# Two output projections by seven quarter products instead of eight, and the last grid sums spread by PE

## The reference, cut to what matters

```python
# first block
mix = concatenate([na_out, ml_out], -1)        # 2048 x 1024: grid attention | mLSTM, 512 columns each
h   = x + gate * (mix @ w_out)                 # w_out 1024 x 1024
x1  = rmsnorm(h, final_norm_w)
# second block
hn  = rms_norm(x1, norm_w_2)                   # feeds the second block's projections
...
mixed = concatenate([y_f, y_a], -1) @ w_out_2  # y_f = fourier part * silu, y_a = dilated attention part
out = x1 + mixed
```

## Time and profile before

| | us |
|---|---|
| median of three runs | 3999.92 |
| profiled execution | 3991.84 |
| its span | 3990.0 |
| PE busy | 3648.1 (91%) |
| ACT, DVE, POOL busy | 1190.5, 921.9, 287.9 |
| first output projection, first matmul to last transpose | 1670.2 to 1926.9 |
| second output projection, first matmul to last | 3763.0 to 3985.2 |

### The profile page before, as it was taken

The page is one execution under the profiler, slowest core; times in us unless marked ns, Lnnn a source line. Parts: engine busy times, 40 slices in busy tenths (PEclk is TensorE's granted clock), DMA queues, the critical chain, the costliest instruction groups (busy, mean ns, idle before and its releaser), DMA issues. The chain is left out here.

```text
span 3990.0 us, 43121 instructions
## 1 busy us (share of the span) xinstructions
PE 3648.1 (91%) x17008; PEld 1955.1 (49%) x17008; DVE 921.9 (23%) x2342; ACT 1190.5 (30%) x2510; POOL 287.9 (7%) x232
## 2 busy tenths in 40 slices
PE   6398888989799999899899999999999999799899
PEld 3147483848354554444354445545454544344444
DVE  2323233232221321322122112222122212111110
ACT  3213131312231331322233445345444544211000
POOL 0101001010200000011000030003000200110000
PEclk9699898989899999999999999999999999899999
DMA  6110010000301101222140475334435604522221
GB/s 221 22 32 22 23 27 23 27 23 21 84 17 35 30 17 19 86 92 82 49 17 11 17 56 17 6 17 61 16 7 24 49 16 12 57 87 83 85 74 63
DMA packets 296935, 172.39 MB, mean 43 GB/s; under 512 B 162793, under 2 KB 263544, under 8 KB 293626
## 3 DMA queue, kind: packets, MB, share of 16 engines
q1 hardware_dynamic: 290470, 159.17, 26.2%
q10 hardware_dynamic: 6272, 10.49, 0.7%
HBM read 147.92 MB, written 21.71 MB: 43 GB/s over the span
## 5 line engine op out<-in xcount | busy, mean ns | idle before, releaser
L1702 PE MATMUL d<-hT,w 128*128 128x512 f32 x2560 | 1121.9, 594 | 8.3 <-POOL qk_w L1692 8.3
L1702 PEld LDWEIGHTS d<-hT,w 128*128 128x128 f32 x2560 | 485.1, 190 | 612.3 <-issue 602.1
L957 PE MATMUL n<-hT,wo 128*128 128x512 f32 x1024 | 454.2, 602 | 22.4 <-issue 12.0
L563 PE MATMUL m<-hT,w 128*128 128x512 f32 x768 | 341.2, 608 | 35.2 <-PEq L473 18.8
L957 PEld LDWEIGHTS n<-hT,wo 128*128 128x128 f32 x1024 | 194.8, 193 | 261.4 <-issue 249.3
L563 PEld LDWEIGHTS m<-hT,w 128*128 128x128 f32 x768 | 149.5, 195 | 224.9 <-issue 224.9
L2108 PE MATMUL f<-hT,w 128*128 128x512 f32 x512 | 222.9, 596 | 22.5 <-PEq L76 18.6
L568 PEld LDWEIGHTS m<-w,hT 128*128 128x128 f32 x2048 | 229.3, 192 | 1.9 <-issue 1.9
L568 PE MATMUL m<-w,hT 128*128 128x128 f32 x2048 | 229.3, 275 | 0.0
L1905 DVE CUSTOM_DVE_ANT_0 sneg<-d,bias 128x192 f32<-128x192 f32 (+1 forms) x384 | 109.5, 323 | 351.0 <-PE d L1736 341.3
L1865 ACT ACTIVATE sq<-d 128x512 f32<-128x512 f32 x96 | 57.2, 596 | 413.2 <-PE d L1702 413.2
(11 more groups left out here) (265 smaller groups left out, 3663.2 us busy)
## 6 DMA issues: line engine op xcount, KB each, us to landing
w<-in_w_in SPq DMA_DIRECT2D x68, 512.0 KB, 3.9
trig<-in_trig SPq DMA_DIRECT2D x16, 1024.0 KB, 5.0
ada<-in_w_ada SPq DMA_DIRECT2D x6, 2048.0 KB, 18.6
xg<-in_x ACTq DMA_DIRECT2D x4, 2048.0 KB, 24.3
rb<-r_rows SPq DMA_DIRECT2D x16, 512.0 KB, 5.5
wo<-in_w_in SPq DMA_DIRECT2D x16, 512.0 KB, 3.9
mix_ml<-in_x SPq DMA_DIRECT2D x16, 512.0 KB, 4.6
x<-mix_ml SPq DMA_DIRECT2D x16, 512.0 KB, 3.0
```

The lines of the kernel that those rows point to most:

```text
L563: last = nc.tensor.matmul(bank[n % 2][:], w[:, s % O_, k], hT[:, k, (n % 4) * TB:(n % 4 + 1) * TB], start=(k == 0), stop=(k == KC - 1))
L957: last = nc.tensor.matmul(bank[b][:], w[:, s, k], hT[:, k, tb * TB:(tb + 1) * TB], start=(k == 0), stop=(k == KC - 1))
L1702: last = nc.tensor.matmul(bank[tb][:], w[:, s, k], hT[:, k, tb * TB:(tb + 1) * TB], start=(k == 0), stop=(k == KC - 1))
```

## The change

Both projections go over pairs of tiles. A pair is A = (A11 A12; A21 A22) with the rows of tile 2j above and of tile 2j+1 below, the mLSTM (or dilated) columns left and the grid (or Fourier) columns right; B is the weight matrix in quarters of 512x512. The seven products, each four matmuls of 128x128 by 128x512, are

```diff
 class GridTail:
+    def widen(self, nc, pool):
+        pool.wait_ge(self.inv_out, 1)
+        wide = self.vT.rearrange("p (u q) -> p u q", q=h2)
+        nc.gpsimd.tensor_tensor(wide, self.fold[:, :].unsqueeze(1).broadcast_to([P, NU, h2]), self.inv[:, :].unsqueeze(2).broadcast_to([P, NU, h2]), ALU.mult).then_inc(self.inv_wide, 1)
+    def scale_last(self, nc, dve, mix, bank):
+        for c in range(NA_CG):
+            dve.wait_ge(self.inverse, c + 1)
+            nc.vector.tensor_tensor(dst, dst, src, ALU.mult).then_inc(self.scaled, 1)
+        for cols in (slice(0, TB), slice(TB, T)):
+            nc.vector.tensor_tensor(mix[:, g, cols], self.o[:, cols], mix[:, g, cols], ALU.mult).then_inc(self.mixed, 1)
 def grid_attention
+                        sp.dma_start(late.fold[:], t["fold"]).then_inc(consts, 16)
+                        sp.dma_start(late.ones[:], t["grid_ones"]).then_inc(consts, 16)
-                store_inverse(PAIRS - 1)
-                pool.wait_ge(consts, 16 * 7)        # the same on PE and ACT
+                pool.wait_ge(consts, 16 * 9)
+                pool.wait_ge(v_turned, 8 * PAIRS)
+                late.widen(nc, pool)
+                        elif g == PAIRS - 1:        # DVE, ahead of the last two write_out
+                            dve.wait_ge(exped, NU * PAIRS)
+                            nc.vector.reciprocal(late.inv[:], total[:]).then_inc(late.inv_out, 1)
 def project_first: SP
-                late.load_inverse(sp, t, PAIRS - 1)
+                sp.dma_start(gate_b[:], t["gate_row"][0, :].partition_broadcast(P)).then_inc(gate_in, 16)
                 (then tiles 0 to 3 of mix_rows and of x, norm_w_2, ident, and final_norm_w once mix_na is whole)
                 for b in range(NT):
                     sp.wait_ge(normed, b + 1)
                     (store b)
+                    if b + NS < NT:
+                        fetch(b + NS)
+                        sp.wait_ge(stored[b % NS], 16 * (b // NS + 1))
+                        sp.wait_ge(scaled, b + 1)
+                        load(b + NS)
 project_first: POOL
-                    nc.gpsimd.tensor_tensor(y[:, b % 2], y[:, b % 2], x[:, b % 2], ALU.add).then_inc(added, 1)
+                pool.wait_ge(gate_in, 16)
+                for k in CHUNKS:
+                    nc.gpsimd.tensor_tensor(w[:, k], w[:, k], gate_b[:], ALU.mult).then_inc(gated, 1)
+                (T3, T2, T4: three tensor_tensor of 128 x 2048)
+                sum_tiles(1)                        # four tensor_tensor of 128 x 512
+                for j in range(1, NJ):
+                    if j + 1 < NJ:
+                        sum_tiles(j + 1)
+                    join(j)                         # three tensor_tensor of 128 x 512
 project_first: PE
+                for c in range(NA_CG):
+                    nc.tensor.matmul(bank[4 + c][:], lhs, late.spread_rows(c), start=True, stop=True).then_inc(late.inverse, 1)
+                for m, k in enumerate(CHUNKS):      # tiles 0 and 1, plain
+                    pe.wait_ge(gated, m + 1)
+                    ...
+                for j in range(1, NJ):
+                    product(j, 1)                   # j == 1 also waits for ys >= 4
+                    turn(2 * j - 2)
+                    product(j, 2)
+                    product(j, 3)
+                    turn(2 * j - 1)
+                    (product(j, 4) to product(j, 7))
+                turn(NT - 2)
+                turn(NT - 1)
 project_first: DVE
+                (x added to the banks of tiles 0 and 1, four times 128 x 512)
+                dve.wait_ge(made, 1)
+                nc.vector.tensor_tensor(B12, B12, B11, ALU.subtract).then_inc(t1_out, 1)
+                norm(0); norm_again(0); norm(1); put(0); norm_again(1)
+                for j in range(1, NJ):
+                    (c11 first, c11, c12 first, c22 first) put(2 * j - 1) (u2, c12) norm(2 * j)
+                    (u3) norm_again(2 * j) (c21) norm(2 * j + 1) put(2 * j) norm_again(2 * j + 1)
 fourier: POOL
+                pool.wait_ge(proj, 8 * PAIRS)
+                tail.make(nc, pool, late)           # waits for wo_in 0 to 7, then T3, T2, T1, T4: 128 x 2048 each
 project_second
+        AHEAD = 3
+        ORDER = [(j, 1) for j in range(AHEAD)]
+        for j in range(NJ):
+            ORDER += [(j, i) for i in range(2, 8)] + ([(j + AHEAD, 1)] if j + AHEAD < NJ else [])
+                tail.collect(nc, act, bank, PAIRS - 1)   # ACT: the Fourier copies of the last pair
+                tail.join(nc, dve, bank, PAIRS - 1)      # DVE: its join, then
+                tail.mix_blocks(nc, dve, mix_f)          # the gate in four pieces of 512
```

More of the change, by code:

```diff
@@ L1230, in project_first, with bank_of, tile_done @@
         out = sem("a_out")
-        stored = [sem("a_stored0"), sem("a_stored1")]
+        stored = [sem(f"a_stored{i}") for i in range(NS)]
+        B11, B12 = w[:, ML:KC, 0:TB], w[:, ML:KC, TB:D]
+        B21, B22 = w[:, 0:ML, 0:TB], w[:, 0:ML, TB:D]
+        T3, T2, T4 = (mixed_w[:, i] for i in range(3))
+        NJ = NT // 2
+        CHUNKS = [0, 1, 2, 4, 5, 6, 7, 3]
+        USED = {1: 1, 2: 2, 3: 4, 4: 5, 5: 6, 6: 7}
+        def bank_of(j, i):
+            return (7 * (j - 1) + i + 3) % 6
+        def tile_done(eng, b):
+            if b < 2:
+                eng.wait_ge(ys, 2 * b + 2)
+            elif b % 2 == 0:
+                eng.wait_ge(held, 7 * (b // 2 - 1) + 6)
+            else:
+                eng.wait_ge(whole, b // 2)
+                eng.wait_ge(joined, 3 * (b // 2))
         with nc.Block() as block:
@@ new lines, in product @@
+                def product(j, i):
+                    a, c = 2 * j, 2 * j + 1
+                    cols = lambda b: [mix_na[:, k, b * P:(b + 1) * P] for k in range(ML)]
+                    ml = lambda b: [stage[:, b % NS, k] for k in range(ML)]
+                    s = lambda m: [sums[:, j % 2, m, k] for k in range(ML)]
+                    done = 4 * (j - 1)
+                    if i == 1:
+                        lhs, rhs = ml(a), B11
+                        pe.wait_ge(fetched[a % NS], 16 * (a // NS + 1))
+                        if j == 1:
+                            pe.wait_ge(late.scaled, PAIRS + 3)
+                            pe.wait_ge(ys, 4)
+                    elif i == 2:
+                        lhs, rhs = cols(a), B21
+                    elif i == 3:
+                        lhs, rhs = s(0), B12
+                        pe.wait_ge(shared_sums, done + 1)
+                        if j == 1:
+                            pe.wait_ge(t1_out, 1)
+                    elif i == 4:
+                        lhs, rhs = s(1), T2
+                        pe.wait_ge(shared_sums, done + 2)
+                        if j == 1:
+                            pe.wait_ge(made, 3)
+                    elif i == 5:
+                        lhs, rhs = s(2), B22
+                        pe.wait_ge(shared_sums, done + 4)
+                    elif i == 6:
+                        lhs, rhs = ml(c), T3
+                    else:
+                        lhs, rhs = cols(c), T4
+                    was = 7 * (j - 1) + i - 7
+                    if was >= 0:
+                        jj, ii = was // 7 + 1, was % 7 + 1
+                        if ii == 7:
+                            pe.wait_ge(whole, jj)
+                        else:
+                            pe.wait_ge(held, 7 * (jj - 1) + USED[ii])
+                    for k in range(ML):
+                        last = nc.tensor.matmul(bank[bank_of(j, i)][:], lhs[k], rhs[:, k], start=(k == 0), stop=(k == ML - 1))
+                    last.then_inc(prod, 1)
@@ L1361, in _ @@
                     nc.vector.reciprocal(st[:, b, 5:6], st[:, b, 4:5]).then_inc(recip, 1)
-                    if b > 0:
-                        put(b - 1)
+                nc.vector.memset(epst[:], EPS).then_inc(once, 1)
+                late.scale_last(nc, dve, mix_na, bank)
+                for b in range(2):
+                    dve.wait_ge(x_in[b], 16)
+                    for n in range(2):
+                        cols = slice(n * TB, (n + 1) * TB)
+                        dve.wait_ge(plain, 2 * b + n + 1)
+                        nc.vector.tensor_tensor(y[:, b, cols], bank[2 * b + n][:], y[:, b, cols], ALU.add).then_inc(ys, 1)
@@ L1393, in _ @@
                 for b in range(NT):
-                    sp.wait_ge(added, 2 * b + 2)
-                    sp.dma_start(y_dst[b], y[:, b % NX]).then_inc(stored[b % NX], 16)
+                    if b % 2 == 0:
+                        sp.wait_ge(held, 7 * (b // 2) + 5)
+                    else:
+                        sp.wait_ge(held, 7 * (b // 2) + 7)
+                        sp.wait_ge(joined, 3 * (b // 2) + 3)
+                    sp.dma_start(y_dst[b], y[b % NX]).then_inc(stored[b % NX], 16)
@@ new lines, in _ @@
+                pe.wait_ge(late.mixed, NTB * PAIRS)
+                for j, i in ORDER:
+                    if (j, i) == (0, 2):
+                        pe.wait_ge(tail.made, 4)
```

(12 more changed lines are left out.)

514 lines of the change are left out of this document (367 added, 147 removed).

## The result

The changed kernel ran in 3929.72 us (median of four runs, 3927.89 to 3934.69), against 3998.49 for the kernel before on the same chip: ratio 0.983, 95% interval 0.9813 to 0.9847, 68.8 us faster. The prediction was 3941, with 3931 to 3954 as its range: the direction and the mechanism of both projections held, the size was too small by 11 us, and the median lies 1.3 us outside the range. The profiled execution took 3927.89 us, span 3926.1.

The account below looks back on a forecast made before the run. PE's own rate was taken to bound both projections. Savings of 30.9 us in the first part and 28.1 in the second, 59 together, took the median from 3999.92 to 3941 us, range 3931 to 3954.

Parts of the forecast that it names:

- Passes: Both projections: 456 and 448 passes for 512 each, at 0.4292 us a pass, saving 24.0 and 27.5 us.
- Steady state: Inside both projections nothing else becomes late for PE; all added waits were costed at nothing.
- rival C: Projections: semaphore waits at each product halve the granted clock; 40% of passes so slowed give median 4096 us; chance 3%.
- rival D: Projections: handing back banks makes PE wait as long as the saved product, gain 8 us, median 3992; chance 1%.
- Grid attention's end and the start: From grid attention's end into the first projection: POOL's chain sets the start, `turn(0)` comes 1.9 us sooner.
- The term for the two more constants: Grid attention's begin: two more DMAs ahead of the complete constants start PE 0.95 us later.
- Rival A: First projection's start: no long DVE/POOL lock, `turn(0)` 5 us sooner, clock holds; gain 65 us, median 3935; chance 13%.
- Second projection's start: End of the Fourier stage: POOL's four weight sums end the block, and PE begins 0.9 us sooner.
- rival B: Both projections' starts: POOL's chains longer, weight sums 5.4 us for 4.5, gate row later; gain 46 us, median 3954; chance 18%.
- The step that failed: Final sum: the median stays 8.1 us above the profiled execution, so 3999.92 less 59 gives 3941 us.

Follow-up runs that it names:

- before_again: The kernel before, unedited, run again; ratio 0.9994 to the kernel before.
- after_again: The changed kernel, unedited, run again; ratio 0.9828 to the kernel before, 69 us faster.
- after_pad24: The changed kernel with 24 one-column matmuls on PE ahead of the first projection's first transposes; ratio 0.9853 to the kernel before.
- first_only: The changed kernel with the old Fourier stage and second projection; ratio 0.9888 to the kernel before, 44.8 us faster.
- before_pad40: The kernel before with 40 one-column matmuls on PE ahead of the first projection's first transposes; ratio 0.9987 to the kernel before.

## Why the prediction was wrong by 11 us, and where it was right

**Passes: right.** 30.3 us from the first to the last turn for 29.9, and 26.5 in the second projection for 27.2; in the pair `before_again` and `after_again` 28.6 and 27.1.

**Steady state: right.** No wait of PE inside a pair; the product cycling of rival C and the banks of rival D cost nothing.

**Grid attention's end and the start: right, with single terms off in both directions.** `widen` took 3.62 us for 4.5; the gate row landed 4.75 us after its issue for 3.7; the gatings took 20.43 us for 21.1. From PE's last work to `turn(0)` it is 48.40 us for 51.47 in the profiled pair, 3.1 saved for 1.9; in `before_again` and `after_again` it is 48.29 for 50.03, 1.7 saved, so the profile of before was long there. The term for the two more constants, -0.95, can't be judged: grid attention's first product comes at 1039.7 in one profile of the changed kernel and at 1044.4 in the other. Rival A fell by T1's 5.50 us; moving T3, T2 and T4 to DVE brought `turn(0)` only 2.5 us nearer to PE's last work, since DVE then has them to do. After its wait of 6.7 us PE ran at half clock for longer in `after_again` than in the profile shown (the eight records behind the transposes took 5.76 us for 4.11), which costs 1.7 us and is the difference between 30.3 and 28.6. Rival A also had the clock hold over a wait of 3.3 us. No run shows that as a rule: in the changed kernel the granted clock was 0.5 from 1659.2 to 1662.6, behind a wait of PE of 2.2 us.

**Second projection's start: right.** +0.6 for +0.9, POOL the last engine; rival B's slower chains were not seen (4.50 us in every sum).

**The step that failed: the last one, "The median of the runs is 8.1 us above it, so 3999.92 - 59 = 3941."** It took the gap between the profiled execution and the median as a constant that the changed kernel would have too, and with it every stage outside the change as equal in both. The changed kernel's gap was 1.8 us. The gap is scatter: over the runs here the profiled execution lies anywhere from 9.5 us below (`after_pad24`) to 11.9 us above (`first_only`) the median of its kernel's others. The profiled execution of before was a short one: its dilated stage took 1501.8 us, where four others in which nothing ahead of that stage was edited on PE took 1514.9 to 1517.8. The changed kernel's nine profiles (with its variants, flat left out) lie at 1497.0 to 1510.6, mean 1503.6. So by these profiles the median of before held some 10 us of waiting for scattered statistics stores which the change happens to take away, though it touches nothing there, and which the prediction had at nothing. By the numbers: 11.3 us of error are 6.3 from the gap that closed, and 4.9 by which the profiled pair itself exceeds 59 (2.2 before grid attention, 1.9 to `turn(0)`, 0.4 to the last turn, 1.5 in the dilated stage and its begin, less 1.1 behind it). That the miss is no larger is partly luck: with that stage made quiet the change is worth 53.5 us, 5.5 less than the sum of its terms, and the stage that was left out brought more than the whole miss.

**What is shown and what is open.** Shown: the excess disappears with contiguous stores (53.5 us), appears in the old kernel by instructions of no use ahead of the dilated stage, and not by the same behind it. Open: how PE's stream sets the length of a stage that waits on SP's stores, and whether the fetches' places decide it. The profiles, one execution each, can't settle it: the dilated stage took 1501.8 and 1517.3 us in two executions of the kernel before, and 1500.4 and 1505.7 in two of the changed one.

## What to carry to other kernels

Before a difference of a profiled execution is carried to the median, ask which stage makes the executions differ, here the one whose PE waits end on DMAs of 4-byte packets. That stage's scatter belongs in the range, and its length is not the same in a kernel edited elsewhere. Repair such a stage first: the contiguous stores were worth 35 us in the kernel before and 20 in the changed one. And a product removed from a bound PE is worth its 3.43 us (eight of them less in the second projection gave 26.5 to 27.1 us), while the weight sums that it needs at its start should stand on the engine that is idle and does them faster, here DVE (2.29 us for 4.50).

## What the runs showed of the hardware that I had not expected

- Sixteen one-column matmuls in a wait of PE made a kernel 12 us faster (0.997), 9 to 12 of it in the stages behind, of which the first begins 230 us later; with contiguous stores there (0.9923 for 0.9913) they gained nothing.
- Four stores of 4 KB in 4-byte pieces, issued behind four like them, hold SP for 17.30 us, in 64-byte rows for 2.51; from the first of the eight to the load behind them pass 36 to 43 us, or 8.
- A float32 matmul of one column is two records and took 0.22 us at a granted clock of 1.00 and 0.43 at 0.50. In `before_pad40` the clock fell to 0.50 at 1701.0, 2.2 us into the run of them and without any wait of PE.
- A DVE operation of 2.29 us began 1.16 us into a POOL one of 4.51 and took 5.50.
